# Where the low parts of the tokens begin in SBUF: remainders by 256 bytes in a kernel of split fp32 products

## The reference, cut to what matters

```
for l in range(2):
    x = layernorm(ALPHA * x + 0.5 * swiglu(x, ffn1_w_in[l], ffn1_w_out[l]))
    x = layernorm(ALPHA * x + hybrid_mixer(x, l, ...))
    x = layernorm(ALPHA * x + 0.5 * swiglu(x, ffn2_w_in[l], ffn2_w_out[l]))
```

## Time and profile before

| what | value |
|---|---|
| median of three runs | 1984.0 us |
| the profiled execution | 1982.76 us |
| its span, first to last instruction | 1981.0 us |
| matmuls of PE | 14178, busy 99% of the span |
| busy: VectorE, ScalarE, GpSimd | 70%, 55%, 8% |
| mean granted clock of TensorE | 0.998 |
| memory traffic | 179 GB/s in the mean |

### The profile page before, as it was taken

The page is one execution under the profiler, slowest core; times in us unless marked ns, Lnnn a source line. Parts: engine busy times, 40 slices in busy tenths (PEclk is TensorE's granted clock), DMA queues, the critical chain, the costliest instruction groups (busy, mean ns, idle before and its releaser), DMA issues.

```text
span 1981.0 us, 35361 instructions
## 1 busy us (share of the span) xinstructions
PE 1958.2 (99%) x14178; PEld 1796.0 (91%) x14178; DVE 1395.6 (70%) x2098; ACT 1095.6 (55%) x1761; POOL 149.7 (8%) x150
## 2 busy tenths in 40 slices
PE   8999999999999999999999999999999999999998
PEld 7889899899988889998999989998888989899996
DVE  7877688746566686778875656657678677886555
ACT  6687476534444577658544444444568756753442
POOL 1200000000000002710000000000000370000000
PEclk9999999999999999999999999999999999999999
DMA  8544467545745544643645755575454564464563
GB/s 283 164 136 136 165 196 235 197 131 195 262 161 170 170 139 150 203 157 130 226 148 192 254 170 163 195 259 175 149 170 129 166 197 149 150 213 149 191 213 126
DMA packets 272891, 354.71 MB, mean 179 GB/s; under 512 B 10211, under 2 KB 226045, under 8 KB 272765
## 3 DMA queue, kind: packets, MB, share of 16 engines
q1 hardware_dynamic: 271421, 348.71, 53.6%
q0 software_dynamic: 1344, 4.23, 0.8%
HBM read 351.83 MB, written 1.08 MB: 178 GB/s over the span
## 4 chain that ended last, share of the span: by engine, by line
PE 87%; DVE 6%; ACT 4%; issue 2%; DMA 1%; POOL 0%; SPq 0%; DVEq 0%; ACTq 0%
PE ps L809 24%; PE ps L811 16%; PE ps L818 16%; PE ps L819 7%; PE ps L813 7%; PE ps L803 3%; PE ps L804 3%; PE ps L805 3%; DVE ring_r L1973 2%; ACT ring_hi L1463 1%; PE ps L1338 1%; DVE tok_r L1973 1%; PE ps L1269 1%; PE ps L1061 1%; ACT tok L1895 1%
## 5 line engine op out<-in xcount | busy, mean ns | idle before, releaser
L1973 DVE TENSOR_TENSOR ring_r<-ring,ring_hi 128x1024 fp32r<-128x1024 f32 x602 | 732.2, 1225 | 386.8 <-ACT ring_hi L1463 384.8
L1463 ACT ACTIVATE ring_hi<-ring 128x1024 fp32r<-128x1024 f32 x602 | 631.8, 1059 | 561.4 <-PE ps L818 341.9
L809 PE MATMUL ps<-xT_hi,ring_hi 128*128 128x256 f32 x2784 | 665.2, 281 | 0.8 <-DVE xT_r L1973 0.8
L811 PE MATMUL ps<-xT_r,ring_hi 128*128 128x256 f32 x2784 | 654.9, 278 | 0.0
L809 PEld LDWEIGHTS ps<-xT_hi,ring_hi 128*128 128x128 f32 x2784 | 524.4, 188 | 16.4 <-issue 11.6
L811 PEld LDWEIGHTS ps<-xT_r,ring_hi 128*128 128x128 f32 x2784 | 524.7, 188 | 0.1
L818 PE MATMUL ps<-xT_hi,ring_r 128*128 128x256 f32 x2784 | 374.7, 277 | 0.0
L818 PEld LDWEIGHTS ps<-xT_hi,ring_r 128*128 128x128 f32 x2784 | 343.6, 188 | 0.0
L2747 POOL TENSOR_TENSOR small<-small,const 128x1 f32<-128x1 f32 (+3 forms) x32 | 39.7, 1241 | 1793.4 <-DVE small L2422 1237.8
L813 PE MATMUL ps<-ring_hi,tok_r 128*128 128x512 f32 x344 | 133.9, 389 | 0.0
L809 PE MATMUL ps<-ring_hi,xT_hi 128*128 128x512 f32 x328 | 130.8, 399 | 1.2 <-DVE tok_r L1973 0.9
(11 more groups left out here) (380 smaller groups left out, 2857.2 us busy)
## 6 DMA issues: line engine op xcount, KB each, us to landing
ring<-in_w_mix_in SPq DMA_DIRECT2D x88, 1024.0 KB, 5.2
ring<-in_ffn_w_in SPq DMA_DIRECT2D x80, 1024.0 KB, 5.1
ring<-in_ffn_w_out SPq DMA_DIRECT2D x44, 1024.0 KB, 4.9
ring<-in_w_branch SPq DMA_DIRECT2D x24, 1024.0 KB, 5.3
ring<-in_w_ffn_up SPq DMA_DIRECT2D x22, 1024.0 KB, 5.1
ring<-in_w_in SPq DMA_DIRECT2D x21, 1024.0 KB, 5.1
ring<-in_w_ffn_down SPq DMA_DIRECT2D x11, 1024.0 KB, 5.1
ring<-in_w_mix_out SPq DMA_DIRECT2D x8, 1024.0 KB, 6.0
```

Source lines behind the costliest of these rows:

```text
L809: pe.matmul(out_, stat[0], mov[0], start=first, stop=False)
L811: pe.matmul(out_, stat[0], mov[1], start=False, stop=False)
L1463: act.activation(half_of(high_of(s), s, q), half_of(ring[:, s % SLOTS, :], s, q), ACT.Copy).then_inc(w_hi, 1)
L1973: return dve.tensor_tensor(lo, whole, hi.bitcast(F32), ALU.subtract)
```

## The change

The padding buffer apart goes. xT, qT and qcT are no longer buffers of their own but three parts of one buffer, lows, that stands ahead of x; the first of them begins 5 floats (20 bytes) into it, and the buffer is 24608 bytes long, 32 more than the three parts, as long as apart and they were together. tok becomes 64 floats (256 bytes) longer, and zT begins 45 floats (180 bytes) later in it than before. mT, h2 and the staged part of tok stay where they were in tok. Nothing else is changed: the instructions, their order and their waits are the same.

```
--- before.py
+++ after.py
@@ -343,18 +343,19 @@
         ring, ring_lo = both("ring", [P, SLOTS, SLOT])
         ring_hi = sb("ring_hi", [P, HIGHS, SLOT], F32R)
         wide, wide_r = both("wide", [P, 24, TOK])
-        tok, tok_r = both("tok", [P, 3 * T * D])
+        tok, tok_r = both("tok", [P, 3 * T * D + 64])
         const, const_r = both("const", [P, CONST_W])
-        sb("apart", [P, 8])
+        LOW_AT = 5
+        lows, lows_r = both("lows", [P, 3 * KD * TOK + 8])
+        xT, qT, qcT = (lows[:, LOW_AT + i * KD * TOK:LOW_AT + (i + 1) * KD * TOK].rearrange("p (k n) -> p k n", n=TOK) for i in range(3))
+        xT_lo, qT_r, qcT_r = (lows_r[:, LOW_AT + i * KD * TOK:LOW_AT + (i + 1) * KD * TOK].rearrange("p (k n) -> p k n", n=TOK) for i in range(3))
         x = sb("x", [P, T, D])
         xT_hi = sb("xT_hi", [P, KD, TOK], F32R)
-        xT, xT_lo = both("xT", [P, KD, TOK])
-        qT, qT_r = both("qT", [P, KD, TOK])
         kT, kT_r = both("kT", [P, KD, TOK])
         xbc, xbc_r = both("xbc", [P, N_XBC, TOK])
-        qcT, qcT_r = both("qcT", [P, KD, TOK])
         kcT, kcT_r = both("kcT", [P, KD, TOK])
         vc_, vc_r = both("vc", [P, T * D])
+        Z_AT = 45
 
         def rows_of(a):
             return a.rearrange("p (t n) -> p t n", t=T)
@@ -365,11 +366,11 @@
         vc = rows_of(vc_[:, :])
         xhat = vc
         gb = qT[:, :, :].rearrange("p a n -> p (a n)").rearrange("p (t n) -> p t n", t=2)
-        tok1 = tok[:, :].rearrange("p (t n) -> p t n", t=T)
+        tok1 = tok[:, 0:3 * T * D].rearrange("p (t n) -> p t n", t=T)
         qa, ka, va = (rows_of(tok[:, i * T * D:(i + 1) * T * D]) for i in range(3))
         oA, xs = qa, ka
-        mT, zT = (feats_of(tok[:, i * T * D:(i + 1) * T * D]) for i in (1, 2))
-        mT_lo, zT_lo = (feats_of(tok_r[:, i * T * D:(i + 1) * T * D]) for i in (1, 2))
+        mT, mT_lo = (feats_of(a[:, T * D:2 * T * D]) for a in (tok, tok_r))
+        zT, zT_lo = (feats_of(a[:, 2 * T * D + Z_AT:3 * T * D + Z_AT]) for a in (tok, tok_r))
         h2, h2_lo, h2_hi = feats_of(tok[:, 0:KF * TOK]), feats_of(tok_r[:, 0:KF * TOK]), wide_r[:, 0:KF, :]
         o1T = feats_of(vc_[:, :])
         memT = wide[:, 16:24, :]
```

## The result

The median after the change is 2012.1 us (2009.3 to 2019.2, five runs), against 1986.2 us (1982.0 to 1988.4, five runs) for the kernel before: a ratio of 1.0138, 95% interval 1.0122 to 1.0154. The change makes the kernel 1.4% slower. I had put faster at 0.55 with 1967 us, and the measured time lies outside my range.

What follows compares the result with a forecast made beforehand. The prediction took matmul count times pace as the bound. Gains of 14.3 (alternating passes), 1.1 (second branch) and 1.6 (slow stretches) made 17.0 us off 1982.8, 1965.8; the median, 1.2 above, was forecast at 1967 us, range 1945 to 2003.

Steps and rivals of the forecast that it cites:

- What bounds the kernel: Whole kernel: time is the number of matmuls times their pace; almost nothing waits for data, largest group wait 0.8 us.
- Alternating passes: Matmuls with high and low token parts in turn: 3168 low-part matmuls gain 4.5 ns each, 14.3 us.
- The bound above: Alternating passes: worst case is the slow rhythm, 113.3 to 117.8 ns, a loss of 28.5 us.
- The slower rival: Hand-over from high to low part costs 0.11 us a half: 2006 us, with the mixers up to 2027; chance 0.28.
- Second branch: Second branch, zT moved: 2.79 to 2.72 us a half, 16 halves in two layers, 1.1 us gained.
- Slow stretches: First block's gates and both mixers, 144 halves: a tenth of 15.8 us, 1.6 us gained, from 0 to 8.
- Low passes: Matmuls of L818, high part alone: high part and weights keep their remainders, so 0.
- Rows mode, staged rows, other engines: Products with xT stationary (bound 6.6 us), staged rows (bound 2.6 us either side), VectorE's writes: each put at 0.
- The two rules: Skill pages: independent read ports would make relative addresses cost nothing; crossings of 16-byte lines would make low streams worse.
- 2.75 or more the slower case: Sign in the first FFN: successive L818 runs 2.75 us or more apart, from 2.72, would show the slower case.
- if the L818 runs themselves change: Sign in the low passes: a change from 1.07 us would show that placing the effect in the hand-over was wrong.

Runs made afterwards that it cites:

- the scan: Kernels issuing only streams of matmuls at varied operand addresses, from several entries, without the reference's work; at h = -64, d = 0 entries settled at 113.3 or 117.8 ns.
- d = 0 at h = -64: Changed kernel with low parts 0, not 12, bytes from high parts by 256 (d), tokens 64 below weights (h): 1984.7 us, ratio 0.9995 to the kernel before.
- h = +112: Kernel with all token parts off the border, moved to 112 bytes above the weights by 256, on a 16-byte border: 1980.95 us, ratio 0.9985 to the kernel before.
- d = -16 and -64: Two kernels: the change with low parts 16 or 64 bytes below the high ones by 256, in place of 12: 2005.4 us (one run) and 2010.6 us.

## Why the prediction was wrong, point by point

**What bounds the kernel** held: the time is matmuls times pace, no wait of PE moved by as much as 1 us, and the edit acted through the pace alone. One reading was off: the earlier trace rows itself has a wait of 1.2 us, not 0.8, as the largest of its groups. Nothing hung on it.

**Alternating passes** is the step that failed. I took "4.5 ns for the low-part matmuls alone", a gain of 14.3 us, on the thought that the surcharge of 6.7 ns comes from a common beat that an offset stream leaves. The runs show the reverse: the alternating passes lost 22.9 us. 113.3 is the lowest pace seen: none of some 90 settings scanned in fp32r went below it, and with 128 columns to load it came at equal remainders of high and low part alone (though at few distances from the weights). Of the 229 fast halves 132 lost 0.05 us (both parts near 116.7) and 95 lost 0.14 (near 119.3). I had leaned on the transposes, whose 2 ns stand over two clocks a column; a stream of one clock a column doesn't reach that.

**The bound above** was right in kind and too low in size. I let the loss end at the slow rhythm, 117.8 ns; the change reaches 119.3 in the kernel and 120.0 in the scan. The slower rival named the place (the hand-over from high to low part) and the price of 0.11 us a half. It is 0.05 in one rhythm and 0.14 in the other, 17.0 us over the 204 halves of the FFNs where the rival had 22.4, and 26.2 over all. That its 2006 to 2027 us holds the result is partly chance: the price is a mixture of two rhythms that the rival didn't have, and the rival named no border, whose share in the loss is open. I had argued it down to 0.28 by saying that in the second branch the equality of low part and weights was to blame. With zT moved off that remainder the branch still takes 2.77 (layer 1) and 2.86 (layer 2), so that equality isn't needed for the excess. But with d = 0 at h = -64 it takes 2.83, and 2.72 only at h = +112. So this row was a true warning, but by itself it could prove neither reading.

**Second branch**: wrong sign. -1.1 us forecast for 2.79 to 2.72; its tokens alone give +0.5 us over both layers, and in the kernel after its 16 halves grew by 0.4. What failed here is the 2.72: I put the branch into the fast rhythm of its neighbour, and it took 2.77 or 2.86 at d = -12 and 2.83 at d = 0.

**Slow stretches**: wrong sign. A gain of 1.6 us was forecast; the 144 halves of the gates and mixers grew by 7.6 us. Some became shorter, by up to 0.09 us; none reached 2.72.

**Low passes** at 0: half right. 1.07 us long where PE is in the faster rhythm, 1.11 where it isn't, although the operands of the low pass didn't move against each other: it runs in the rhythm of the pass ahead of it. That makes 3.3 us, start to start.

**Rows mode, staged rows, other engines** at 0: right. The 512-column groups of the earlier trace rows moved by under 1 us each, VectorE by 0.1 us.

**The two rules.** The scans measure both. A start off a 16-byte border costs the moving stream 3 to 7 ns of 113.3, and no distance scanned brings it back to 113.3 (the lowest is 115.5, at h = -20 and +28). The Trainium skill, "SBUF — State Buffer" (Specifications), with its 16-byte lines and its price for each crossing, pointed the right way, and the trace agrees for fp32r moving operands; it doesn't for the stationary operand or for bf16, where no price shows. At h = 0 the pace is 120.0 with 128 columns to load and 113.3 in most entries with 16. The Trainium skill's rule of two independent read ports ("TensorE: Matmul & The Clock Gate", Part 2, step 1) would have the distance between the two operands cost nothing; in these runs it costs up to 6%. The third price, of d, is there on a border too (d = -16 and -64).

Of the signs that I named, "2.75 or more the slower case" appeared at once, and "if the L818 runs themselves change" did so in part of the kernel.

What stays open: what in the chip makes the difference of two successive moving streams cost, and why an entry picks one rhythm; and how the change's loss divides between border and difference. Both are present in it. d alone, on a border, costs 22 us (-16, one run) or 25 (-64). The border alone I estimate from the scan at 3168 x 6.7 ns = 21 us, for low parts at 120.0. The two would make 43 to 46 us and the change loses 26.5, so they don't simply add. No full kernel has the border alone with every distance kept: with all tokens off the border h moved too.

## What to carry to other kernels

In this kernel, where PE is busy 99% of the time with fp32r products, its operands' starts cost up to 2.5%. Keep moving streams on a 16-byte border and high and low parts at one remainder by 256. The distance to the weights matters as much: on a border and with d = 0 the pace is 113.3 ns in most or all entries at -64 or +112 and 116.7 to 120.0 at most others. Measure such a distance with a stream of some 30 matmuls from several entries, because the same addresses have two steady paces and one entry shows only one of them. And where a profile holds a single stretch that already has the property to be introduced (here the second branch), give it more weight than a mechanism for which no row speaks, and ask how it was entered.

## What the runs showed of the hardware that I had not expected

- One set of addresses has two steady paces, 113.3 and 117.8 ns, kept over dozens of matmuls; at h = -64, d = 0 six and two of eight entries had them. What in the entry picks isn't shown.
- Paces lie between 113.3 and 123.3 ns, with single entries at 126.7 and 130.0, and 4 bytes can move a stream by several ns: d = -4 has 116.7, -8 120.1, -12 mostly 120.0, -16 118.3.
- A matmul whose own operands haven't moved gets slower when its neighbour's have: from the start of a high part's matmul to the next start, 3168 of them took 9.7 us more in the kernel after. A slow rhythm is also carried on: the third branch at d = 0 went from 2.72 to 2.83 us a half behind a second branch in a slower rhythm.
- bf16 streams of the same shape have 109.2 ns at all four settings tried, 4 ns under the lowest pace of fp32r, and show none of its surcharges there.
